# Mixed values turned by VectorE's 32x32 block transposes and by 128-byte stores, instead of on TensorE

## Chip, cores and metric

The kernel runs on one core of a Trainium2 chip. The metric is the device time of one execution in microseconds; a version is told by the median of its runs. All data are f32 (products are made of a high and a low part in a reduced f32 format, three matrix products each).

## What is computed

One layer of a hybrid encoder on 1024 tokens of width 1024. Eight heads of width 128 produce the 1024 mixed values of a token: four heads of gated linear attention (GLA) and four of differential attention. Each head's output is normalised over its 128 values and gated. Then the output projection reads all of them, with the features as the contracted dimension:

```python
o_gla = head_rmsnorm(o_gla, gla_norm_w[l]) * silu(ggate)            # (B, S, 4, 128)
o_diff = head_rmsnorm(o_diff, diff_norm_w[l]) * (1.0 - lam_init) * silu(dgate)
mixed = concatenate([o_gla.reshape(B, S, 512), o_diff.reshape(B, S, 512)], axis=-1)
x = x + mixed @ w_out[l]
hc = rmsnorm(x, norm_cross_w[l])
x = x + cross_attention(hc, rmsnorm(mem, norm_mem_w[l]), w_cq[l], w_ckv[l], w_co[l])
return rmsnorm(x, final_norm_w)
```

## The kernel before

Everything is ordered by one hand-written list, PLAN: `stages()` builds it and `with_weights()` puts the loads of weight tiles between. Each engine walks the whole list and issues its part of every stage, so the order on an engine, and on its DMA queue, is the order of the list. Semaphores tie the engines together.

The tokens are tiled by 128 (TT = 8 tiles). After the gate preparation come GLA_STEPS = 16 steps (two head pairs, eight tiles each), then DIFF_STEPS = 32 steps (four heads, eight tiles each), then the cross-attention keys K and values V of the memory, then the output projection X in seven products of half-size blocks, then the cross attention (Q, SC, PT, O), its output projection Y and the final norm. TensorE projects the next steps' inputs (proj, proja, projb) between the small products of a step, as its filler.

How a mixed value travels. In a GLA step s TensorE leaves the output of a head pair in PSUM (stage o), VectorE sums it into o_f, ScalarE squares it (osq), VectorE and GpSimd make the inverse norm (ovar; POOL's line L997), and VectorE multiplies norm and gate in (stage ofin, L1598) and writes 128 tokens x 256 features to a half of mix_out. SP stores it to the HBM scratch `mixed`, laid out token by feature, in rows of 1 KB (L961). mix_out has two halves, so ofin(s) waits for the store of step s-2. A differential step i does the same with 128 x 128 values (PV, pvvar, pvfin at L1696, L967, rows of 512 bytes) and four quarters of mix_out.

The output projection wants features on the partitions. So from the last quarter of the differential steps on, ScalarE's queue loads `mixed` back, a tile of 128 tokens x 512 features at a time (stage loadm, L1362, into one of two halves of tile_a, rows of 2 KB), TensorE transposes it in four 128x128 pieces into a PSUM bank (stage MT, by `turn`, L1932), and ScalarE copies the bank to mixT, scaled by the head norm's weight (L1111). There are 16 such tiles: MT(t, 0) of the GLA features and MT(t, 1) of the differential ones. The tile MT(t, 0) stands between proja and proj of a differential step from i = 22 on, seven of them; the nine others stand between the K and V stages. loadm of tile n + 2 stands directly behind MT of tile n. xa stages then split mixT into high and low parts, and asum stages add blocks of it, on VectorE and by GpSimd's accumulating DMAs.

Other users of the queues: SP's queue also loads every weight tile (w, L921, 256 KB, a ring of four raw tiles and 13 split ones) and the residual tiles (loadx); GpSimd's queue adds up blocks of the output weights in HBM during the GLA steps (out_sums, one 1 MB transfer per step for 11 steps, issued behind the inverse norm) and of the cross output weights during the differential steps (late_sums, every second step).

On VectorE a GLA step is, in order: sc_lo (stage sc), the state and its low part (kv), var_o (ovar), q_lo and k_lo (qk), ke_lo (kdT), ofin of the step before, v and gate of the next projection (proj, gmul), w_lo of a weight tile, the masked scores (scp), o_f (o). A differential step is: row maximum of the next scores (max), var_o, the low parts of the transposed map (T) and of the next queries and keys (TQK), pvfin of the step before, w_lo, the map (comb), v, gate and rope of a later projection (proj), pv_f (PV).

Transposes go to PSUM banks in turn, kept in order by `rings`: TR numbers the stages T, MT, HT and PT, TURN_ACT all of them but MT, whose copy is counted by ring_raw. `turned_out` makes TensorE wait until VectorE has read the earlier ones.

Of the kernel before, what the change touches and what calls it, by code (L numbers as in the profile page):

```python
# [32 lines left out]
P = 128  # L33
# [13 lines left out]
NEG = -1e30  # L47

# [79 lines left out]
def stages():  # L128
# [41 lines left out]
    plan.append(("ofin", GLA_STEPS - 1))  # L170
# [12 lines left out]
    for i in range(last):  # L183
# [12 lines left out]
        if i + 3 < DIFF_STEPS:  # L196
# [14 lines left out]
    plan.extend([*turned_maps(last), ("pvvar", last - 1), ("K", 2), ("pvfin", last - 1), ("Ke", 2)])  # L211
    plan.extend(turned_tile(n_turned))
    n_turned += 1
    plan.extend([("K", 3), ("Ke", 3), *turned_tile(n_turned), ("PV", last), ("pvvar", last), ("pvfin", last)])
# [217 lines left out]
TR = rings({"T", "MT", "HT", "PT"})  # L432


TURN_ACT = rings({"T", "HT", "PT"})
# [7 lines left out]
def ring_bank(stage):  # L443

    if stage[0] == "T":
        return 6 + stage[2]
    return 7 if stage[0] == "MT" and not stage[2] else 6 + TR[stage] % 2

# [70 lines left out]
def build(nc, a, out):  # L519

    with ExitStack() as ctx:
# [67 lines left out]
        mix_out = sb("mix_out", [P, 512], F32, part1)  # L589
# [81 lines left out]
        mixed = nc.dram_tensor("mixed", (S, D), F32, kind="Internal").ap()  # L671
# [11 lines left out]
        d_mixg = [sem(f"gla_mix_stored{j}") for j in range(2)]  # L683
        d_mixd = [sem(f"diff_mix_stored{j}") for j in range(4)]
# [45 lines left out]
        ring_raw = sem("mixed_tiles_kept")  # L730
        sum_dve = sem("weight_sums")
# [115 lines left out]

        def ring_job(stage):
# [10 lines left out]
            c = cols(t if kind == "MT" else t % 4)  # L859
# [45 lines left out]
        def _(sp):  # L905
# [39 lines left out]
            for stage in PLAN:  # L945
# [11 lines left out]
                elif kind == "ofin":  # L957
                    s = w[0]
                    p, t = divmod(s, TT)
                    sp.wait_ge(of_dve, at("ofin", s))  # L960
                    sp.dma_start(mixed[cols(t), 256 * p:256 * p + 256],  # L961
                                 mix_out[:, 256 * (s % 2):256 * (s % 2) + 256]).then_inc(d_mixg[s % 2], 16)
                elif kind == "pvfin":
                    i = w[0]
                    h, t = divmod(i, TT)
                    sp.wait_ge(pf_dve, at("pvfin", i))
                    sp.dma_start(mixed[cols(t), GH * GDV + P * h:GH * GDV + P * h + P],  # L967
                                 mix_out[:, P * (i % 4):P * (i % 4) + P]).then_inc(d_mixd[i % 4], 16)
# [1296 lines left out]
```

## Time and profile before

| | us |
|---|---|
| median of 3 runs (824.53 to 827.13) | 825.1 |
| the profiled execution | 825.03 |
| its span | 823.3 |

| engine | busy us | share of the span |
|---|---|---|
| PE (TensorE matmul) | 809.1 | 98% |
| DVE (VectorE) | 574.7 | 70% |
| ACT (ScalarE) | 430.6 | 52% |
| POOL (GpSimd) | 85.7 | 10% |
| DMA queue of SP (q1) | | 24.5% of 16 engines |
| DMA queue of POOL (q0) | | 19.6% of 16 engines |

All times in the profile count from the span's start. A row of a timeline is one instruction or a merged run of equal ones, with its start and duration, and in brackets how long the engine had idled before and who released it. The chain that ended last is followed back from the last instruction, at each step to what released it; an engine that fills the chain is the bound there. The granted clock of TensorE is at its full level over nearly the whole span. The GLA steps run from about 83 to 205 us, the differential ones to 485, K and V to 518, X to about 612.

### The profile page before, as it was taken

The numbers are of one execution on the slowest core, as the hardware profiler recorded it, in microseconds if no ns is written. First come the engines' busy times: TensorE is split into PE (matmuls) and PEld (weight loads), VectorE is DVE, ScalarE is ACT, GpSimd is POOL, SyncE is SP. The second block draws the span as 40 slices with busy tenths as digits, with TensorE's granted clock in tenths as the row PEclk, the third lists the DMA queues.
The fourth block names the chain that finished last, engine by engine and source line by source line (L and its number), as shares of the span: only waits on it lengthen the run. The fifth ranks groups of instructions, "written<-read, shape, count | busy, mean of one in ns | idle before, by whom it ended". The sixth has DMA issues, their size and how long they took to land.

```text
span 823.3 us, 12950 instructions
## 1 busy us (share of the span) xinstructions
PE 809.1 (98%) x4472; PEld 678.9 (82%) x4472; DVE 574.7 (70%) x1330; ACT 430.6 (52%) x1041; POOL 85.7 (10%) x122
## 2 busy tenths in 40 slices
PE   8999999999999999999999999999999999999996
PEld 7878888887788888888888898888888888888885
DVE  6688566665678668767757877599836454367997
ACT  6775445443455445445546576644645454366443
POOL 3100122211010111111000001010110000001201
PEclk9999999999999999999999999999999999999999
DMA  8321369952223255545512178954422111206945
GB/s 292 115 83 39 91 192 205 193 121 65 87 88 109 84 99 109 114 84 122 108 63 74 58 227 248 295 124 124 150 81 77 39 64 52 78 13 143 216 91 204
DMA packets 70408, 99.19 MB, mean 120 GB/s; under 512 B 6596, under 2 KB 38472, under 8 KB 70344
## 3 DMA queue, kind: packets, MB, share of 16 engines
q1 hardware_dynamic: 52360, 64.29, 24.5%
q0 software_dynamic: 15392, 29.36, 19.6%
q10 hardware_dynamic: 2592, 4.72, 1.7%
q8 instruction: 36, 0.59, 0.3%
q14 instruction: 28, 0.23, 0.1%
HBM read 83.68 MB, written 31.46 MB: 140 GB/s over the span
## 4 chain that ended last, share of the span: by engine, by line
PE 90%; DVE 7%; ACT 2%; issue 1%; DMA 0%; POOL 0%; ACTq 0%; DVEq 0%
PE bank L1860 14%; PE bank L1862 14%; PE bank L1861 14%; PE banks2to L1860 10%; PE banks2to L1862 10%; PE banks2to L1861 10%; PE banks6to L1932 4%; PE banks2to L2126 3%; PE bank L2149 2%; DVE neg_max L1659 2%; DVE w_lo L1395 1%; PE banks2to L2066 1%; PE bank L2151 1%; DVE prT_lo L1394 1%; DVE actT_lo L1394 1%
## 5 line engine op out<-in xcount | busy, mean ns | idle before, releaser
L1862 PE MATMUL bank<-w_hi,actT_lo 128*128 128x512 f32 x412 | 161.4, 392 | 0.0
L1860 PE MATMUL bank<-w_hi,actT_hi 128*128 128x512 f32 x384 | 154.9, 403 | 0.7 <-DVE gate L1549 0.4
L1861 PE MATMUL bank<-w_lo,actT_hi 128*128 128x512 f32 x384 | 149.6, 390 | 0.0
L1395 DVE SCALAR_TENSOR_TENSOR w_lo<-w_raw,vecs,w_hi 128x512 fp32r<-128x512 f32 x120 | 86.8, 749 | 27.2 <-ACT w_hi L1111 27.2
L1862 PEld LDWEIGHTS bank<-w_hi,actT_lo 128*128 128x128 f32 x412 | 77.3, 188 | 17.1
L1111 ACT ACTIVATE w_hi<-w_raw,vecs 128x512 fp32r<-128x512 f32 x120 | 82.5, 720 | 7.1 <-DMA w_raw<-in_w_ckv 3.8
L1860 PEld LDWEIGHTS bank<-w_hi,actT_hi 128*128 128x128 f32 x384 | 72.1, 188 | 16.2 <-DVE w_lo L1395 1.5
L1861 PEld LDWEIGHTS bank<-w_lo,actT_hi 128*128 128x128 f32 x384 | 72.3, 188 | 12.9
L997 POOL TENSOR_TENSOR rs_o<-var_o,neg_half 128x1 f32<-128x1 f32 (+1 forms) x48 | 31.1, 647 | 369.1 <-DVE var_o L1686 256.8
L1862 PE MATMUL banks2to<-w_hi,actT_lo 128*128 128x512 f32 x164 | 64.0, 390 | 0.0
L1278 ACT ACTIVATE prob<-banks2to,neg_maxs 128x128 f32<-128x128 f32 (+7 forms) x64 | 46.9, 740 | 15.1 <-DVE neg_maxs L1660 15.0
L1111 ACT ACTIVATE w_hi<-w_raw 128x512 fp32r<-128x512 f32 x56 | 33.8, 627 | 36.5 <-DMA w_raw<-out_sums 13.3
L1659 DVE TENSOR_REDUCE neg_max<-banks2to 128x2 f32<-128x256 f32 (+8 forms) x33 | 43.4, 1316 | 4.4 <-PE banks2to L2131 4.0
L1860 PE MATMUL banks2to<-w_hi,actT_hi 128*128 128x512 f32 x112 | 44.7, 399 | 0.0
L1861 PE MATMUL banks2to<-w_lo,actT_hi 128*128 128x512 f32 x112 | 43.7, 390 | 0.0
L1394 DVE TENSOR_TENSOR w_lo<-w_raw,w_hi 128x512 fp32r<-128x512 f32 x56 | 37.2, 685 | 9.0 <-ACT w_hi L1111 9.0
L1860 PE MATMUL banks2to<-actT_hi,w_hi 128*128 128x512 f32 (+1 forms) x100 | 39.6, 396 | 1.6 <-DVE w_lo L1395 1.6
L1111 ACT ACTIVATE qk_tok<-bank 128x192 f32<-128x192 f32 x27 | 8.9, 331 | 56.9 <-PE bank L1862 56.9
L1812 DVE TENSOR_REDUCE x_negmax<-banks2to 128x4 f32<-128x1024 f32 x8 | 9.8, 1223 | 41.1 <-PE banks2to L1862 41.1
L1862 PE MATMUL banks2to<-actT_hi,w_lo 128*128 128x512 f32 (+1 forms) x100 | 38.3, 383 | 0.0
L1861 PE MATMUL banks2to<-actT_lo,w_hi 128*128 128x512 f32 (+1 forms) x100 | 38.2, 382 | 0.0
L2149 PE MATMUL bank<-dv,prT_hi 128*128 128x256 f32 x144 | 35.3, 325 | 1.4 <-DVE qkT_lo L1394 0.7
(373 smaller groups left out, 2009.7 us busy)
## 6 DMA issues: line engine op xcount, KB each, us to landing
w_raw<-in_w_in SPq DMA_DIRECT2D x56, 256.0 KB, 3.8
out_sums<-in_w_out POOLq DMA_DIRECT2D x11, 1024.0 KB, 10.0
late_sums<-in_w_co POOLq DMA_DIRECT2D x11, 1024.0 KB, 9.0
w_raw<-in_w_ckv SPq DMA_DIRECT2D x32, 256.0 KB, 3.4
w_raw<-in_w_cq SPq DMA_DIRECT2D x32, 256.0 KB, 2.7
stage_in<-in_x SPq DMA_DIRECT2D x8, 512.0 KB, 4.6
tile_a<-mixed ACTq DMA_DIRECT2D x16, 256.0 KB, 3.4
x_res<-in_x SPq DMA_DIRECT2D x8, 512.0 KB, 6.8
```

Of the source, the lines that this page charges most:

```text
L997: pool.tensor_tensor(dst, src, neg_half[:, 0:n], ALU.pow).then_inc(sem_out, 1)
L1111: return act.activation(dst, src, ACT.Copy, scale=scale)
L1278: last = act.activation(prob[:, m, 0:n], wide[:, 2 * m:2 * m + 2, :].rearrange("p j c -> p (j c)")[:, 0:n], ACT.Exp, scale=DQK ** -0.5, bi ...
L1394: return dve.tensor_tensor(dst, src, hi.bitcast(F32), ALU.subtract)
L1395: return dve.scalar_tensor_tensor(dst, src, scale, hi.bitcast(F32), ALU.mult, ALU.subtract)
L1659: then_wait(dve.tensor_reduce(neg_max[:, i % 2, m], both[:, m, :], AX.X, ALU.max, negate=True))
L1860: pe.matmul(dst, l_hi, r_hi, start=start, stop=False)
L1861: pe.matmul(dst, l_hi, r_lo, start=False, stop=False)
L1862: return pe.matmul(dst, l_lo, r_hi, start=False, stop=stop)
L1932: last = pe.transpose(ps[:, cols(j)], src, ident[:, :])
L2126: last = pe.matmul(wide[:, 2 * half + g // 512, 0:keys.stop - g], l[rows, 0, cols(t)], r[rows, 1, keys], start=m == 0, stop=m == 2 and key ...
L2149: pe.matmul(bank1[:, 0:256], prT_hi[:, b, :], dv2[:, v, :, :].rearrange("p a c -> p (a c)"), start=b == 0, stop=False)
```

## The change

The scratch `mixed` is laid out feature by token. Behind each ofin and pvfin there is a new stage, oturn or pvturn: VectorE turns the product within 32x32 blocks into the new tile mix_t, and SP stores it in four transfers, one for each band of 32 partitions (32 tokens). In a transfer, row r of block b goes to feature 32 b + r, and its 32 tokens are a run of 128 bytes in HBM. A GLA step stores 1024 such runs, a differential step 512, where 128 rows were stored before. mix_out and mix_t have 256 columns each, where mix_out had 512. For GLA both are one buffer: ofin(s) waits for oturn(s-1), and oturn(s) for the landed store of step s-1. For the differential steps both have two.

oturn(s-2) stands behind sc(s), pvturn(i-1) ahead of PV(i). At the end of the GLA steps the order is oturn(14), ofin(15), oturn(15). The tile MT is loaded as 512 rows of 512 bytes, already turned, and ScalarE copies it from tile_a to mixT; TensorE has no part in MT any more, and the rings number T, HT and PT alone.

```diff
+BLK = 32
+STORED = 16 * P // BLK
...
         plan.append(("sc", s))
+        plan.extend([("oturn", s - 2)] if s > 1 else [])
...
-    plan.append(("ofin", GLA_STEPS - 1))
+    plan.extend([("oturn", GLA_STEPS - 2), ("ofin", GLA_STEPS - 1), ("oturn", GLA_STEPS - 1)])
...
+        plan.extend([("pvturn", i - 1)] if i else [])
         if i == last - 2:
...
-TR = rings({"T", "MT", "HT", "PT"})
-TURN_ACT = rings({"T", "HT", "PT"})
+TR = rings({"T", "HT", "PT"})
...
-        mix_out = sb("mix_out", [P, 512], F32, part1)
+        mix_out = sb("mix_out", [P, 256], F32, part1)
+        mix_t = sb("mix_t", [P, 256], F32, part1)
...
-        mixed = nc.dram_tensor("mixed", (S, D), F32, kind="Internal").ap()
+        mixed = nc.dram_tensor("mixed", (D, S), F32, kind="Internal").ap()
...
+        def turned_rows(first, n, t, band):
+            tokens = slice(P * t + BLK * band, P * t + BLK * band + BLK)
+            return mixed[first:first + n, tokens].rearrange("(b r) c -> r b c", r=BLK)
+        def turned_blocks(first, n, band):
+            return mix_t[BLK * band:BLK * band + BLK, first:first + n].rearrange("r (b c) -> r b c", c=BLK)
...
 SP:
-                elif kind == "ofin":
+                elif kind == "oturn":
                     s = w[0]
                     p, t = divmod(s, TT)
-                    sp.wait_ge(of_dve, at("ofin", s))
-                    sp.dma_start(mixed[cols(t), 256 * p:256 * p + 256],
-                                 mix_out[:, 256 * (s % 2):256 * (s % 2) + 256]).then_inc(d_mixg[s % 2], 16)
+                    sp.wait_ge(mg_dve, s + 1)
+                    for a4 in range(P // BLK):
+                        sp.dma_start(turned_rows(256 * p, 256, t, a4),
+                                     turned_blocks(0, 256, a4)).then_inc(d_mixg, 16)
 (pvfin becomes pvturn in the same way, with d_mixd[i % 2])
...
                 elif kind == "loadx":
                     if w[0] == 4:
-                        sp.wait_ge(pf_dve, DIFF_STEPS)
+                        sp.wait_ge(md_dve, DIFF_STEPS)
...
 ScalarE, MT:
-                    act.wait_ge(ring_pe, TR[stage] + 1)
+                    act.wait_ge(d_tile[n % 2], 16 * (n // 2 + 1))
...
+                    loaded = tile_a[:, 512 * (n % 2):512 * (n % 2) + 512].rearrange("p (j c) -> p j c", j=4)
+                    copy(mixT[:, 4 * kk:4 * kk + 4, cols(t)], loaded,
...
 ScalarE, loadm:
-                        act.wait_ge(ring_pe, TR[RELOADS[n - 2]] + 1)
+                        act.wait_ge(ring_raw, n - 1)
...
+                    rows = mixed[512 * kk:512 * kk + 512, cols(t)].rearrange("(j p) c -> p j c", p=P)
...
 VectorE:
                 elif kind == "ofin":
-                    if s >= 2:
-                        dve.wait_ge(d_mixg[j], 16 * (s // 2))
+                    wait(dve, mg_dve, s)
...
+                elif kind == "oturn":
+                    s = w[0]
+                    dve.wait_ge(of_dve, s + 1)
+                    wait(dve, d_mixg, STORED * s)
+                    dve.transpose(mix_t[:, :], mix_out[:, :]).then_inc(mg_dve, 1)
+                elif kind == "pvturn":
+                    i = w[0]
+                    dve.wait_ge(pf_dve, i + 1)
+                    if i < 2:
+                        dve.wait_ge(d_mixg, STORED * GLA_STEPS)
+                    else:
+                        dve.wait_ge(d_mixd[i % 2], STORED * (i // 2))
+                    dve.transpose(mix_t[:, cols(i % 2)], mix_out[:, cols(i % 2)]).then_inc(md_dve, 1)
...
 TensorE:
-                elif kind == "MT":
-                    n = RELOAD[stage]
-                    pe.wait_ge(d_tile[n % 2], 16 * (n // 2 + 1))
-                    turn(stage, [tile_a[:, cols(4 * (n % 2) + j)] for j in range(4)])
```

## Rows read from the trace of the kernel before

**Rows 1.** The page: busy time of TensorE, and the chain's shares by engine.

```profile
PE 809.1 (98%) x4472; PEld 678.9 (82%) x4472; DVE 574.7 (70%) x1330; ACT 430.6 (52%) x1041; POOL 85.7 (10%) x122
...
PE 90%; DVE 7%; ACT 2%; issue 1%; DMA 0%; POOL 0%; ACTq 0%; DVEq 0%
```

**Rows 2.** Busy time by stretch: GLA steps, 130 to 170 us, differential steps, keys and values.

```profile
core 0: us, PE busy (x) PEld busy (x) DVE busy (x) ACT busy (x) POOL busy (x), PEclk, DMA share, GB/s
90.00:210.00 120.00, 118.97 (x668) 98.25 (x668) 76.21 (x237) 53.92 (x189) 23.61 (x27) 1.00 0.67 150
130.00:170.00 40.00, 39.38 (x229) 32.65 (x228) 25.94 (x81) 18.14 (x62) 9.90 (x11) 1.00 1.01 195
210.00:485.00 275.00, 272.73 (x1698) 229.08 (x1697) 200.04 (x586) 141.92 (x411) 27.10 (x43) 1.00 0.41 98
485.00:515.00 30.00, 30.00 (x176) 26.02 (x175) 23.89 (x35) 20.09 (x36) 2.65 (x2) 1.00 0.81 250
```

**Rows 3.** DMA queues (packets, MB, share): 130 to 170 us, then 180 to 220.

```profile
q0 software_dynamic: 2741, 5.42, 80.2%
q1 hardware_dynamic: 4018, 2.35, 20.5%
...
q1 hardware_dynamic: 3755, 2.10, 19.2%
```

**Rows 4.** The chain in order of time: start us, us charged, what (a stage MT).

```profile
442.74 0.44 PE banks6to L1932 x4
```

**Rows 5.** VectorE's timeline in a differential step.

```profile
448.25 1.76 DVE L1659 TENSOR_REDUCE neg_max<-banks2to 128x2 f32<-128x1536 f32 x1 [0.17 <-PE banks2to L2131]
```

**Rows 6.** ScalarE's copies of MT, and the landing of their loads.

```profile
L1111 ACT ACTIVATE mixT<-banks6to,scale_neg x8: 670/682/704, 401.0 to 515.1; 128x512 f32<-128x512 f32 x8
...
DMA to landing us min/median/max: 2.5/3.4/6.8
```

**Rows 7.** VectorE's timeline in a GLA step.

```profile
124.38 0.42 DVE L1394 TENSOR_TENSOR v<-bank,v 128x256 fp32r<-128x256 f32 x1 [1.36 <-ACT tanh_g L1186]
...
128.57 0.28 DVE L1394 TENSOR_TENSOR q_lo<-q_dec,q_hi 128x128 fp32r<-128x128 f32 x1
...
129.67 0.61 DVE L1598 SCALAR_TENSOR_TENSOR mix_out<-o_f,rs_o,gate 128x128 f32<-128x128 f32 x2 [0.61 <-POOL rs_o L997]
131.52 0.42 DVE L1394 TENSOR_TENSOR v<-bank,v 128x256 fp32r<-128x256 f32 x1 [1.24 <-ACT tanh_g L1186]
```

**Rows 8.** The chain in order of time, two long differential steps.

```profile
385.45 0.34 DVE pv_f L1680
...
457.72 2.04 DVE neg_max L1659
```

**Rows 9.** Landing of stores into mixed: 90-165, 165-210, 210-490 us; those of 101.1, 145.0.

```profile
DMA to landing us min/median/max: 2.4/5.9/11.3
...
DMA to landing us min/median/max: 1.8/1.8/5.1
...
DMA to landing us min/median/max: 1.6/1.6/9.5
...
DMA to landing us min/median/max: 6.3/6.3/6.3
...
DMA to landing us min/median/max: 6.5/6.5/6.5
```

**Rows 10.** SP's issue of a transfer in pieces of 64 bytes (duration in ns).

```profile
L938 SPq DMA_DIRECT2D ga_raw<-in_w_in x1: 447/447/447, 5.8 to 5.8; - x1
```

**Rows 11.** VectorE's and TensorE's timelines at the end of the GLA steps.

```profile
205.04 0.61 DVE L1598 SCALAR_TENSOR_TENSOR mix_out<-o_f,rs_o,gate 128x128 f32<-128x128 f32 x2
205.57 0.41 DVE L1659 TENSOR_REDUCE neg_max<-banks2to 128x2 f32<-128x256 f32 x1
...
209.13 0.42 DVE L1394 TENSOR_TENSOR qkT_lo<-banks6to,qkT_hi 128x256 fp32r<-128x256 f32 x1
...
209.71 0.39 PE L2126 MATMUL banks2to<-qkT_hi 64*128 64x256 f32 x2
```

More of the change, by code:

```diff
@@ L210, in stages @@
             plan.append(("PV", i))
-    plan.extend([*turned_maps(last), ("pvvar", last - 1), ("K", 2), ("pvfin", last - 1), ("Ke", 2)])
+    plan.extend([*turned_maps(last), ("pvvar", last - 1), ("K", 2), ("pvfin", last - 1), ("Ke", 2), ("pvturn", last - 1)])
     plan.extend(turned_tile(n_turned))
     n_turned += 1
-    plan.extend([("K", 3), ("Ke", 3), *turned_tile(n_turned), ("PV", last), ("pvvar", last), ("pvfin", last)])
+    plan.extend([("K", 3), ("Ke", 3), *turned_tile(n_turned), ("PV", last), ("pvvar", last), ("pvfin", last), ("pvturn", last)])
     n_turned += 1
@@ L446, in ring_bank @@
         return 6 + stage[2]
-    return 7 if stage[0] == "MT" and not stage[2] else 6 + TR[stage] % 2
+    return 6 + TR[stage] % 2
 RELOADS = [stage for stage in PLAN if stage[0] == "MT"]
@@ L682, in build @@
         d_raw = [sem(f"weight_loaded{j}") for j in range(NRAW)]
-        d_mixg = [sem(f"gla_mix_stored{j}") for j in range(2)]
-        d_mixd = [sem(f"diff_mix_stored{j}") for j in range(4)]
+        d_mixg = sem("gla_mix_stored")
+        d_mixd = [sem(f"diff_mix_stored{j}") for j in range(2)]
         d_tile = [sem(f"mixed_tile_loaded{j}") for j in range(2)]
@@ L1690, in _ @@
                     dve.wait_ge(pv_pool, i + 1)
[L1691 to L1692 removed]
+                    if i < 2:
+                        dve.wait_ge(mg_dve, GLA_STEPS)
                     else:
[L1694 removed]
+                        dve.wait_ge(md_dve, i - 1)
                     c = slice(P * (i % 4), P * (i % 4) + P)
[L1696 removed]
+                    dve.scalar_tensor_tensor(mix_out[:, cols(i % 2)], pv_f[:, i % 2, :], rs_o[:, i % 2, 0:1], gate[:, c],
                                              ALU.mult, ALU.mult).then_inc(pf_dve, 1)
@@ L1908, in late_bank @@
                 return banks[LATE_BANK[stage]]
-            kept = [0]
             def turned_out(n):
-                mixed_tiles = sum(stage[0] == "MT" for stage in list(TR)[:n])
-                wait(pe, ring_dve, n - mixed_tiles)
-                if mixed_tiles > kept[0]:
-                    kept[0] = mixed_tiles
-                    pe.wait_ge(ring_raw, mixed_tiles)
+                wait(pe, ring_dve, n)
             def turn(stage, parts):
@@ L2196, in _ @@
                     open_already = kind == "Q" and ("Qa", *w) in NTH
-                    pe.wait_ge(ring_dve, TURN_ACT[("HT", 4 * half + 3, 0 if kind == "Qa" and h + d == 0 else 1)] + 1)
+                    pe.wait_ge(ring_dve, TR[("HT", 4 * half + 3, 0 if kind == "Qa" and h + d == 0 else 1)] + 1)
                     ps = banks[LATE_BANK[job]] if open_already else late_bank(job)
```

39 lines of the change are left out of this document (16 added, 23 removed).

## The prediction

> **What bounds the kernel now.** I read the page from the top. TensorE is busy 98% of the span, and the chain that ended last is TensorE for 90% and VectorE for 7% [rows 1]. The table by stage shows how little it idles: 118.97 of 120 us busy in the GLA steps, 272.73 of 275 in the differential ones, 30.00 of 30 while the memory keys and values are projected [rows 2]. So TensorE work that goes away is time saved, as long as nothing else becomes late by as much, and VectorE is the only engine that already is late here and there. The DMA engines matter for what follows: 0.67 of them are busy over the GLA steps and 1.01 from 130 to 170 us, where GpSimd's queue alone holds 80.2% and SP's 20.5% [rows 2, 3].
>
> The sum is made against the profiled execution: 825.03 us, span 823.3 and 1.7 around it. The median of the runs is 825.1, so the two are the same for this purpose.
>
> **Removed: the transposes on TensorE.** Sixteen MT stages of four 128x128 transposes go. Transposes overlap their neighbours, so I don't take their durations but what the chain of work charges TensorE for one stage of four, 0.44 us [rows 4]. 16 x 0.44 = 7.0 us. Nine of them lie behind 475 us, where TensorE is busy all the time; seven lie from 400 to 452 us, and in the last three of these steps VectorE has only 0.17 us idle ahead of a row maximum [rows 5]. There I count nothing for three, so 13 x 0.44 = **-5.7 us** (-3.5 to -7.0).
>
> **MT on ScalarE.** The copy reads SBUF instead of PSUM (0.68 us before [rows 6], SBUF hardly slower) and waits for the load itself; the next load waits for that copy. This puts some 0.4 us of idle into ScalarE per tile, 14 times. ScalarE is busy 20 of 30 us there [rows 2], so I cost it at nothing. If that cover were gone it would be up to 14 x 0.4 = 5.6 us. The reload keeps its bytes with 512 pieces of 512 bytes in place of 128 of 2 KB; it landed in 2.5 to 6.8 us [rows 6], with two stages of the fill between issue and use. Nothing, with up to 1 us as the other end.
>
> **Added on VectorE, differential steps.** A pvturn per step, one 128x128 instruction. The trace has no block transpose; the nearest rows are subtractions, 0.28 us for 128x128 and 0.42 for 128x256 [rows 7]. I take 0.3 (0.15 to 1.2: half of it, and four passes). In most steps it falls into idle time before the row maximum. Where the step is long it doesn't: the chain of 384 to 391 us runs through VectorE's rope sum, the reduction pv_f, ScalarE's square of it, w_hi, w_lo and the maximum without a gap [rows 8], and pvturn stands exactly ahead of pv_f. The same chain comes at this step of the two heads before, near 250 and 318 us, and the maximum at 457.72 starts one that holds to 470, with two pvturns on it. 5 x 0.3 = **+1.5 us** (+0.5 to +6). Stores here have two buffers, so a store has two steps to land in; the slowest took 9.5 us [rows 9], and 32 steps in 275 us are 8.6 each. No wait.
>
> **Added at the end of the GLA steps.** ofin(15) needs mix_out free, so oturn(14) stands directly ahead of it, and oturn(15) directly behind must wait until the store of step 14 has landed in HBM, since mix_t has one buffer. SP issues four transfers for it: 0.45 us each (the nearest issue of short pieces took 0.447), and a store landed 1.8 us after issue at this quiet place [rows 9, 10]. From 205.04 us, where ofin stood, that is 0.42 for oturn(14), 3 x 0.45 + 1.8 = 3.15 until the last transfer has landed, and 0.42 for oturn(15): VectorE comes to max(0) at 209.0 instead of 205.57, 3.5 us late. Queued behind it are max(0), E(0) on ScalarE, comb(0) and the lo part of the next keys at 209.13. TensorE starts S(1) at 209.71, 0.16 us after that lo part ends, with its filler used up [rows 11]. So nearly all of it shows: **+3.5 us** (+1.5 to +7).
>
> **Added in each GLA step.** This is the term in doubt. Before, mix_out had two halves and a store two steps. Now oturn(s) waits until the store of step s-1 has landed, one step earlier. A step is 7.1 us (the values of two projections start at 124.38 and 131.52). Behind oturn VectorE still does the state, the lo parts and ofin until 130.3, then idles 1.24 us until the values of the next projection [rows 7]. Less 0.42 for the transpose, 0.8 us of delay is free; beyond that v, gate and with them TensorE's next products slip. So a store may take 7.1 + 0.8 from one oturn to the next. It takes 0.42 + 3 x 0.45 + its landing, so a landing above 6.2 us is paid for. Before, ten stores from 90 to 165 us landed in 2.4 to 11.3 us, median 5.9, the other six mostly in 1.8 [rows 9]. Issued one by one, three took 6.2 to 6.3, one, the longest, 11.3 and the next 6.5 [rows 9]; with nothing added these are 0.1 + 0.1 + 5.1 + 0.3 = 5.6 us over the limit. Then there are 64 pieces per DMA engine and step instead of 8. SP's pieces took 19.2% of 16 x 40 us / 3755 = 33 ns at a mean of 560 bytes from 180 to 220 us [rows 3]; in proportion to bytes that is 8 ns for one of 128, at most the same 33: 0.5 to 2.1 us, less 0.3 for the eight that go. With 0.7 each, the five are 9 us over it. Against that, a step that slips lets GpSimd's stream drain. I take **+6 us**, near the lower of the two (0 if the new place of the stores, 3 us earlier in the step, misses the stream; up to 20 below).
>
> The Trainium skill, in "DMA: Bandwidth & Descriptors" under Specifications, puts a line at 512 bytes for full rate, below which a DMA engine reads, modifies and writes. That speaks against this change: its pieces are 128 bytes in place of 512 and 1024. No row here shows a store below 512 bytes. The slow-store rival below is what it would do.
>
> **SP's queue.** A step's store is four issues, 4 x 0.45 = 1.8 us in place of one, and stands behind sc (GLA) or proj (differential), ahead of the weight loads that follow in the plan; the wait for VectorE that SP does there delays them too. In a GLA step one weight tile is loaded, and the ring is filled tiles ahead, so I cost it at nothing; up to 1.4 us per group change, seven of them, if a load is what VectorE's w_lo waits for.
>
> **Sum.** 825.0 - 5.7 + 1.5 + 3.5 + 6 = **830.3 us**, its own range 826 to 837.
>
> **The rivals.**
> 1. *The stores hide.* oturn never waits in a GLA step; only the end of these steps and the transposes are paid. 825.0 - 5.7 + 1.5 + 3.5 = 824.3 us (822.6 to 827). For it: landings of 2.4 to 4.3 in four of ten stores. Against: the DMA engines are full from 130 to 170 us.
> 2. *Faster: TensorE's share comes back whole.* Also the wait behind oturn(14) is short or covered and transposes cost 0.2: 825.0 - 7.0 + 1.0 + 1.0 = 820.0 us. It decides if S(1) has slack or SP issues the four in a fraction of 0.45. Against: TensorE starts S(1) within 0.2 us of its operand [rows 11].
> 3. *Short pieces are slow.* From 130 to 170 us a piece of GpSimd's stream took 80.2% of 16 x 40 / 2741 = 187 ns [rows 3]. If each short piece has to let one of these pass, 64 x 0.19 = 12 us per step in place of 7.1 + 0.8, so about 4 us over six steps, 24, and the early steps some more in part; the same follows if a piece of 128 bytes costs several times its share. 824.3 + 24 = 848 us.
> 4. *It does not do what it says*: the TensorE rows with tile_a stay in number before 515 us. The edits delete them, so no chance is kept for it.
>
> **How the numbers follow.** The forecast 0.43, rival 1 0.28, rival 2 0.12, rival 3 0.17. A change below 0.3% (2.5 us: 822.6 to 827.6) can't be told from none. Faster: rival 2 whole and 0.06 of rival 1, 0.18. Same: 0.21 of rival 1 and 0.04 of the forecast, 0.25. Slower: 0.57. The range 821 to 846 leaves out half of each outer rival.
>
> **What would show it.** The four transposes per MT gone and TensorE busy about 7 us less. VectorE idle ahead of its transposes, released by the DMA into mixed: about 3 us once near 205 us, and some of 1 to 5 us from 100 to 180 us; without these, rival 1. The stretch from the first GLA step to 210 us longer by 4 to 10 us, the stretch from 475 to 520 shorter by some 4. The transpose at 0.3 and 0.42 us. Landing of the new stores: below 6 us everywhere speaks for rival 1, above 10 in most steps for rival 3. The forecast is wrong if TensorE's idle time in the GLA steps grows by less than 3 us or more than 15.

## The result, and the profile after

The changed kernel takes 837.8 us (median; 835.2 to 838.5), the kernel before 824.9 in the same rounds: ratio 1.0147, 95% interval 1.0135 to 1.0159. The forecast was 830.3, range 821 to 846. The sign was right, the size was not: 12.1 us (1.0147 x 824.9 - 824.9) where 5.3 were forecast. TensorE has 64 instructions fewer [rows 1] and the span is still 12.8 us longer. From the page of the changed kernel, the busy times and the chain:

```profile
PE 807.5 (97%) x4408; PEld 675.7 (81%) x4408; DVE 585.2 (70%) x1378; ACT 431.0 (52%) x1041; POOL 85.8 (10%) x122
...
PE 82%; DVE 8%; DMA 4%; ACT 3%; issue 2%; SPq 1%; ACTq 0%; DVEq 0%
```

TensorE's busy time fell by 1.6 us, not by 7, and the chain of waits now has 4% of DMA in it. The table by stretch (columns as in [rows 2]; the last stretch is 5 us longer):

```profile
90.00:210.00 120.00, 112.79 (x622) 93.46 (x621) 76.81 (x235) 52.44 (x179) 23.64 (x27) 0.97 0.71 148
130.00:170.00 40.00, 34.16 (x184) 28.03 (x182) 22.54 (x69) 14.93 (x50) 9.40 (x10) 0.91 0.96 177
210.00:485.00 275.00, 269.17 (x1621) 223.66 (x1621) 202.15 (x619) 135.09 (x403) 26.04 (x41) 0.99 0.41 90
485.00:520.00 35.00, 32.85 (x212) 28.84 (x210) 26.27 (x45) 25.45 (x46) 2.45 (x3) 1.00 0.72 209
```

TensorE idles 5.8 of 40 us where it idled 0.6, the granted clock is 0.91 there instead of 1.00, and it now idles 2.15 us while the memory keys and values are projected.

**Where the time goes, by marks.** The order of the work is the same in both kernels, so the same instruction can be looked up in both, and the difference of its starts says how late the changed kernel is at that point. VectorE's timeline (start us, duration, ...): in the kernel before, the values of the last GLA projection, the third row maximum, the 24th, the last, and the first variance behind the output projection:

```profile
190.01 0.42 DVE L1394 TENSOR_TENSOR v<-bank,v 128x256 fp32r<-128x256 f32 x1 [1.27 <-ACT tanh_g L1186]
218.45 0.95 DVE L1659 TENSOR_REDUCE neg_max<-banks2to 128x2 f32<-128x768 f32 x1
396.25 2.29 DVE L1659 TENSOR_REDUCE neg_max<-banks2to 128x2 f32<-128x2048 f32 x1 [0.68 <-PE banks2to L2131]
467.17 1.21 DVE L1659 TENSOR_REDUCE neg_max<-banks2to 128x1 f32<-128x1024 f32 x1
591.04 0.14 DVE L1807 TENSOR_SCALAR var_x<-sq_x 128x1 f32<-128x1 f32 x1
```

and the same five in the changed kernel:

```profile
198.76 0.42 DVE L1409 TENSOR_TENSOR v<-bank,v 128x256 fp32r<-128x256 f32 x1 [0.45 <-ACT tanh_g L1200]
232.27 0.95 DVE L1686 TENSOR_REDUCE neg_max<-banks2to 128x2 f32<-128x768 f32 x1
410.57 2.29 DVE L1686 TENSOR_REDUCE neg_max<-banks2to 128x2 f32<-128x2048 f32 x1 [0.49 <-PE banks2to L2148]
478.13 1.22 DVE L1686 TENSOR_REDUCE neg_max<-banks2to 128x1 f32<-128x1024 f32 x1
603.88 0.14 DVE L1834 TENSOR_SCALAR var_x<-sq_x 128x1 f32<-128x1 f32 x1
```

The differences are 8.75, 13.82, 14.32, 10.96 and 12.84 us, so the five stretches cost +8.75, +5.07, +0.50, -3.36 and +1.88. From there to the last instruction nothing changes in any run; in e1 and e12 below the span ends 0.9 us later behind that instruction than in the others, which no mark shows.

| stretch | forecast | measured |
|---|---|---|
| GLA steps (to 190 us) | +6 | +8.75 |
| end of GLA, first maxima (to 218) | +3.5 | +5.07 |
| 22 differential steps (to 396) | +1.5 with the next | +0.50 |
| steps with seven reloads (to 467) | 4 x -0.44 = -1.76 | -3.36 |
| keys, values, output projection (to 591) | 9 x -0.44 = -3.96 | +1.88 |

(The forecast's four and nine are stages at 0.44 us; behind 475 us it counted only them.) The largest miss is the last row, 5.8 us; the first two together miss 4.3.

**The waits.** VectorE's waits of the changed kernel (us in total, times, the longest):

```profile
DVE mix_t L1619 <- DMA mixed<-mix_t: 13.9, 4, 7.3
```

Its 16 GLA transposes by their line (duration in ns, min, median, max):

```profile
L1619 DVE STREAM_TRANSPOSE mix_t<-mix_out x16: 435/438/446, 97.8 to 217.6; 128x256 f32<-128x256 f32 x16
```

Two of the four that waited for a store, from the timeline:

```profile
149.51 0.45 DVE L1619 STREAM_TRANSPOSE mix_t<-mix_out 128x256 f32<-128x256 f32 x1 [7.31 <-DMA mixed<-mix_t]
217.57 0.45 DVE L1619 STREAM_TRANSPOSE mix_t<-mix_out 128x256 f32<-128x256 f32 x1 [2.27 <-DMA mixed<-mix_t]
```

The other two waits were 1.98 us at 121.81 and 2.30 at 188.65. Over the first of these the values stay within 0.91 us of the kernel before, over the one of 7.31 they go from 0.36 to 6.34 us late, over the last from 8.05 to 9.25 and back to 8.75. The store that the transpose at 149.51 waits for lies in the stretch from 130 to 150 us. The DMA queues there (packets, MB, share), then the landing of SP's stores:

```profile
q0 software_dynamic: 1317, 2.60, 72.5%
q1 hardware_dynamic: 4288, 1.31, 30.3%
```

```profile
DMA to landing us min/median/max: 1.5/9.4/11.1
```

GpSimd's queue holds 72.5% of the 16 engines, and SP's pieces fill the rest.

**The clock.** What I had not counted is that TensorE is slow behind these stalls. Its timeline at the second row maximum, then the table by stretch around both stalls:

```profile
218.12 0.39 PE L1889 MATMUL bank<-w_hi,actT_lo 128*128 128x512 f32 x1
221.94 0.39 PE L2143 MATMUL banks2to<-qkT_hi 64*128 64x256 f32 x2 [3.43 <-DVE qkT_lo L1409]
...
223.16 0.63 PE L1888 MATMUL banks2to<-w_lo,actT_hi 128*128 128x512 f32 x1
```

```profile
152.00:157.00 5.00, 4.45 (x17) 3.63 (x17) 4.02 (x12) 2.31 (x8) 1.39 (x2) 0.50 0.64 92
...
218.00:222.00 4.00, 0.57 (x5) 0.15 (x3) 2.41 (x11) 2.25 (x9) 0.00 (x0) 1.00 0.22 35
222.00:226.00 4.00, 4.00 (x17) 3.20 (x18) 2.42 (x10) 1.91 (x6) 0.00 (x0) 0.58 0.24 63
226.00:230.00 4.00, 4.00 (x19) 3.23 (x19) 1.39 (x6) 0.39 (x1) 0.00 (x0) 0.99 0.26 66
```

After 3.43 us of idle the granted clock is 0.5 of full speed (1.2 instead of 2.4 GHz) for some 4 us, and a matmul that took 0.39 us takes 0.63. The second row maximum is 11.27 us late (222.78 against 211.51), the third 13.82. The same follows the stall near 150 us: the values at 146.60 before are 6.34 late, those at 153.65 then 8.04. Here no run holds the clock up, so how much of the 1.7 us is the clock isn't shown. In e8, whose only change lies 60 us later, the same two are 6.97 and 8.12 late.

**Behind 485 us.** The chain of waits from 483 to 530 us in the changed kernel (start, us charged, what; a part of it):

```profile
487.88 4.16 DMA w_raw<-in_w_ckv
492.07 0.74 ACT w_hi L1125
492.83 1.43 DVE w_lo L1410 x2
494.27 6.21 DMA w_raw<-in_w_ckv
...
501.13 0.72 ACT mixT L1125
...
506.13 1.22 DVE mixT L1666
...
509.03 3.71 DMA w_raw<-in_w_ckv
...
517.30 5.35 DMA w_raw<-in_w_ckv
522.67 0.73 ACT w_hi L1125
523.43 0.76 DVE w_lo L1410
524.23 0.50 PE banks2to L1887
```

This is a ring: SP may load a raw weight tile when VectorE has made the lo part of the tile four before, the load takes 3.7 to 6.2 us, ScalarE and VectorE split it, and that frees the next. Between two loads the chain also runs through what stands ahead of the split on these engines: ScalarE's copy of a reloaded tile (mixT, L1125) and VectorE's sum of two blocks (L1666). In the kernel before the chain of this stretch is TensorE from end to end.

### The profile page after: what moved, and what is told of

Same layout as the page of the kernel before. It is cut to its first block, busy times and chain, and to the rows that moved or that the text cites. A ratio compares the mean times of both kernels' runs of the same rounds, so it can differ in the third digit from the quotient of the medians.

```text
span 836.1 us, 13037 instructions
## 1 busy us (share of the span) xinstructions
PE 807.5 (97%) x4408; PEld 675.7 (81%) x4408; DVE 585.2 (70%) x1378; ACT 431.0 (52%) x1041; POOL 85.8 (10%) x122
## 4 chain that ended last, share of the span: by engine, by line
PE 82%; DVE 8%; DMA 4%; ACT 3%; issue 2%; SPq 1%; ACTq 0%; DVEq 0%
PE bank L1887 13%; PE bank L1889 13%; PE bank L1888 13%; PE banks2to L1887 9%; PE banks2to L1889 9%; PE banks2to L1888 9%; PE banks6to L1949 3%; PE banks2to L2143 3%; DMA w_raw<-in_w_ckv 2%; DVE w_lo L1410 2%; PE bank L2166 2%; DMA mixed<-mix_t 1%; DVE neg_max L1686 1%; PE banks2to L2083 1%; PE bank L2168 1%
## 5 line engine op out<-in xcount | busy, mean ns | idle before, releaser
L1125 ACT ACTIVATE w_hi<-w_raw,vecs 128x512 fp32r<-128x512 f32 x120 | 82.8, 720 | 13.0 <-DMA w_raw<-in_w_ckv 9.0
L1125 ACT ACTIVATE w_hi<-w_raw 128x512 fp32r<-128x512 f32 x56 | 33.7, 627 | 37.8 <-DMA w_raw<-out_sums 13.5
L1121 ACT ACTIVATE junk<-pv_f 128x128 bf16<-128x128 f32 x32 | 9.9, 310 | 54.4 <-DVE pv_f L1707 54.4
L1889 PEld LDWEIGHTS banks2to<-w_hi,actT_lo 128*128 128x128 f32 x164 | 31.2, 190 | 6.7
```

Source lines behind the costliest of these rows:

```text
L1125: return act.activation(dst, src, ACT.Copy, scale=scale)
L1889: return pe.matmul(dst, l_lo, r_hi, start=False, stop=stop)
```

## The experiments

The runs of one batch share the runs of the kernel before (825.2, 824.9 and 825.0 us). "Late at the marks" is the difference over the five stretches, as above, in the profiled execution.

| run | median us | ratio, interval | GLA | to 218 | to 396 | to 467 | to 591 |
|---|---|---|---|---|---|---|---|
| changed kernel | 837.8 | 1.0147, 1.0135-1.0159 | +8.75 | +5.07 | +0.50 | -3.36 | +1.88 |
| e1 four buffers | 825.9 | 1.0006, 0.9997-1.0015 | -0.04 | +0.94 | +0.57 | -3.36 | +2.54 |
| e2 long stores | 830.7 | 1.0068, 1.0054-1.0081 | +0.97 | +5.98 | +0.54 | -3.37 | +0.88 |
| e3 long reloads | 836.3 | 1.0126, 1.0111-1.0142 | +8.50 | +5.07 | +0.55 | -3.35 | +1.46 |
| e4 TensorE only | 821.9 | 0.9954, 0.9941-0.9966 | -0.03 | +0.03 | +0.04 | -3.55 | +0.42 |
| e5 GLA values only | 821.8 | 0.9965, 0.9953-0.9978 | 0.00 | 0.00 | +0.01 | -3.54 | -0.25 |
| e6 e4, later rows | 820.2 | 0.9947, 0.9935-0.9959 | +0.02 | -0.01 | +0.04 | -3.54 | -0.92 |
| e7 e4, no reloads | 819.4 | 0.9932, 0.9920-0.9943 | 0.00 | 0.00 | -0.03 | -3.54 | +0.11 |
| e8 busy TensorE | 834.8 | 1.0127, 1.0109-1.0146 | +8.63 | +3.30 | +0.58 | -3.36 | +3.46 |
| e9 no sums | 828.8 | 1.0044, 1.0032-1.0055 | -0.01 | +6.15 | +0.51 | -3.33 | +2.41 |
| e10 whole, mended | 823.0 | 0.9974, 0.9964-0.9984 | 0.00 | 0.00 | +0.58 | -3.35 | +1.66 |
| e11 e5, later rows | 820.7 | 0.9951, 0.9938-0.9963 | 0.00 | 0.00 | +0.01 | -3.55 | -0.31 |
| e12 e1, long late pieces | 824.9 | 1.0001, 0.9992-1.0010 | -0.04 | +0.92 | +0.52 | -3.36 | +0.76 |

The GLA mark is taken from the first GLA step (81.37 us before); up to there a run starts up to 0.6 us earlier or later. Stretches in which two runs do the same agree within 0.1 us, with waits of microseconds in them within 0.3. The last stretch is the exception: runs alike in all that touches it (the changed kernel, e1, e8, e9) give 1.9 to 3.5. So the profiles say nothing there below about 1.5 us, and small differences are read from the medians. The marks are those of one execution, which need not be near the median: that of e8 took 837.1 us, and those of e7, e9 and e10 were the slowest of their runs (821.2, 830.4 and 824.1). In e2, e3, e4, e6, e7, e9 and e12 something is left out or lands elsewhere, so they don't compute the layer; the others do.

### Is it the single buffer, the piece size, or GpSimd's stream?

**e1.** Four buffers for the transposed GLA values:

```
-                    wait(dve, d_mixg, STORED * s)
-                    dve.transpose(mix_t[:, :], mix_out[:, :]).then_inc(mg_dve, 1)
+                    if s >= 4:
+                        dve.wait_ge(d_mixg[s % 4], STORED * (s // 4))
+                    dve.transpose(tile_a[:, 256 * (s % 4):256 * (s % 4) + 256], mix_out[:, :]).then_inc(mg_dve, 1)
```

> The changed kernel with four buffers for the transposed GLA values in place of one (they lie in the SBUF of tile_a, which is unused until the reloads), so that a transpose waits for the store of four steps before; everything else, the 128-byte pieces too, stays. Theory A (the single buffer): the lines of the two traces drift apart by 8.75 us over the GLA steps and by 5.1 us more over the first two row maxima, all of it at transposes that waited for a store and at TensorE's slow stretch right behind them. It goes: 837.8 - 13.8 = 824 us, VectorE has no wait for DMA ahead of a GLA transpose. Rival B (the short pieces load the DMA engines, whatever waits for them): the weights and GpSimd's stream are late too, the GLA steps stay 3 us or more longer than before, 828 to 834 us.

825.9 us: theory A, 12 us back (1.9 us short of the 824 expected; in its profiled execution 0.94 of that lies at the first maxima and 0.9 at the end of the span). The stores from 130 to 150 us land as late as before:

```profile
DMA to landing us min/median/max: 7.8/8.9/10.7
```

Nobody waits for them any longer: VectorE's list of waits from 84 to 225 us has no DMA. SP's issues of these transfers got long too, 0.46 to 5.05 us with a median of 1.74 (0.30 to 2.03 with a median of 0.78 in the changed kernel, both from 130 to 150 us), where the forecast had 0.45 each. The 0.94 us left at the first maxima are about the two transposes ahead of max(0), 2 x 0.44; in e10, which moves them, nothing is left.

**e2.** The same four transfers of a store in long rows:

```
-                        sp.dma_start(turned_rows(256 * p, 256, t, a4),
-                                     turned_blocks(0, 256, a4)).then_inc(d_mixg, 16)
+                        sp.dma_start(mixed[P * t + BLK * a4:P * t + BLK * a4 + BLK, 256 * p:256 * p + 256],
+                                     mix_t[BLK * a4:BLK * a4 + BLK, 0:256]).then_inc(d_mixg, 16)
```

> The changed kernel, but the four transfers of a store write 32 rows of 1 KB (GLA) or 512 bytes (differential) in place of 128-byte pieces: same bytes, same four issues, same single buffer and waits; the values land in another place, so what is computed from them is not the reference's, and the reloads read other rows in pieces of 512 bytes as before. Theory A (a store is late because it is issued behind GpSimd's stream and waited for one step later; the size of its pieces hardly matters): the long wait near 150 us and the one behind oturn(14) stay, 834 to 839 us. Rival B (the small pieces are what takes long): the waits in the GLA steps fall below 1 us in all, 824 to 829 us.

830.7 us, between the two expectations: both are half wrong. VectorE's waits for stores, all of the run:

```profile
DVE mix_t L1619 <- DMA mixed<-mix_t: 7.7, 5, 2.6
```

and the landing of the stores from 130 to 150 us:

```profile
DMA to landing us min/median/max: 2.0/3.5/5.8
```

Five waits and none above 2.6 us where one of 7.3 stood, a median landing of 3.5 us instead of 9.4, and the GLA steps are 0.97 us late, not 8.75: the size of the pieces is most of that term. The end of the GLA steps is no better than with short pieces (+5.98 against +5.07): there the wait is four issues and one landing. VectorE's wait is even a little shorter, 1.89 us against 2.27, but the granted clock stays at 0.50 to 0.71 from 212 to 220 us, where the changed kernel has its low stretch for some 4 us; e9 has the same (+6.15, a wait of 2.03 us, 0.50 to 0.76 from 212 to 220).

**e9.** GpSimd's accumulating transfers left out (and SP's waits for the sums that they would have made), the single buffer and the short pieces kept:

```
-                    if w[0] < len(OUT_ADDENDS):
+                    if w[0] < 4:
```

> The changed kernel without GpSimd's seven accumulating transfers of 1 MB in the GLA steps (the four that start the sums stay; the sums of the output weights are incomplete, so the result is not the reference's). Single buffer, short pieces and waits stay. Theory A2 (a store of 128-byte pieces is only late when it stands in the same DMA engines as GpSimd's stream): nearly all of the 8.75 us of the GLA steps goes, waits of VectorE for a store there below 1 us in all, the 5.1 us at the first two row maxima stay: 837.8 - 8 = 829.5 us, 828.5 to 831. Rival (they are slow by themselves): 834 us or more.

828.8 us, as theory A2 has it. All waits for stores in the run:

```profile
DVE mix_t L1619 <- DMA mixed<-mix_t: 2.0, 1, 2.0
```

The one left is that of oturn(15), and the short pieces land quickly once the stream is gone (130 to 190 us):

```profile
DMA to landing us min/median/max: 1.5/1.7/3.0
```

So the 8.75 us need three things at once: one buffer, pieces of 128 bytes and the stream. Without any one of them they shrink to 1 us or nothing (e1, e2, e9). Two or three buffers were not tried.

### The clock at the end of the GLA steps

**e8.** TensorE kept busy in its idle time:

```
+                    for _ in range(28 * (i == 1)):
+                        pe.transpose(banks[6][:, 0:P], ident[:, :], ident[:, :])
                     pe.wait_ge(tq_dve, i + 1)
```

> The changed kernel with 28 transposes of the identity on TensorE (0.11 us each, 3.1 in all) ahead of the first wait of S(1), in the 3.43 us that TensorE idles near 220 us; nothing reads them. There the granted clock fell to 0.50 for some 4 us after the idle stretch and a matmul of 128x512 took 0.63 instead of 0.39 us. Theory H (the second row maximum is late by 2.55 us more because of this clock): the clock stays at 1.00 and about 2.5 us come back, 835.3 us. Rival: it is late because of what VectorE or ScalarE do, and the time stays at 837.8, or is longer if the transposes end behind the operand.

834.8 us, ratio 1.0127 against 1.0147: 1.6 us back, not 2.5, and the two intervals overlap; the marks decide. The transposes fill the gap, the matmuls behind it keep 0.39 us and the clock stays at 1.00. TensorE's timeline of this run, then its table by stretch:

```profile
217.65 3.22 PE L2133 MATMUL banks6to<-ident 128*128 128x128 f32 x28
221.07 0.39 PE L2145 MATMUL banks2to<-qkT_hi 64*128 64x256 f32 x2 [0.20 <-DVE qkT_lo L1409]
...
222.07 0.39 PE L1888 MATMUL banks2to<-w_lo,actT_hi 128*128 128x512 f32 x1
```

```profile
222.00:226.00 4.00, 4.00 (x21) 3.23 (x20) 2.39 (x8) 2.29 (x7) 0.00 (x0) 1.00 0.09 25
```

The stretch to 218 us falls from 5.07 to 3.30: 1.8 us of it were the clock. The other 3.3 are the wait itself, close to the 3.5 of the forecast. Of the 2.55 us between the second and the third maximum 0.97 stay at full clock (10.40 to 11.37 us late in e8); that part theory H had wrong. The late stretch of this run is the worst of all (+3.46), with the clock at 0.83 from 520 to 530 us; that is why its marks add up to only 0.8 us less than the changed kernel's (12.05 against 12.84).

### Why nine of the sixteen stages gave nothing

**e4.** The kernel before with TensorE's part alone:

```
-                elif kind == "MT":
-                    n = RELOAD[stage]
-                    pe.wait_ge(d_tile[n % 2], 16 * (n // 2 + 1))
-                    turn(stage, [tile_a[:, cols(4 * (n % 2) + j)] for j in range(4)])
```

> The kernel before, with only TensorE's part of the change: the transposes MT are left out and ScalarE copies the reloaded tile as it is (untransposed, so what is computed from it is not the reference's); stores, reloads and VectorE as before. The forecast's term: 13 of 16 stages at 0.44 us, 825 - 5.7 = 819.3 us. Theory D (TensorE runs into the pace of the weights behind 485 us, and only the seven stages before give time): the lines gain 3.3 us by 460 us and nothing or a loss after it, 821 to 822.5 us. Rival E (the loss behind 485 us is made by the stores and their place in SP's queue): the whole share, 818 to 819.5 us.

821.9 us, theory D. Seven stages give 3.55 us, 0.51 each, also the three that the forecast left out because VectorE had 0.17 us of slack [rows 5]; the nine behind give nothing (+0.42). From 500 to 510 us, first the kernel before, then e4, by the table of stretches:

```profile
500.00:510.00 10.00, 10.00 (x48) 8.15 (x47) 8.45 (x13) 6.17 (x12) 1.35 (x1) 1.00 0.86 256
```

```profile
500.00:510.00 10.00, 7.90 (x34) 5.72 (x33) 8.28 (x12) 5.91 (x10) 1.35 (x1) 1.00 1.03 285
```

What ScalarE waits for from 470 to 530 us, first the kernel before, then e4:

```profile
ACT w_hi L1111 <- DMA w_raw<-in_w_ckv: 3.8, 5, 1.4
```

```profile
ACT w_hi L1108 <- DMA w_raw<-in_w_ckv: 8.4, 7, 2.8
```

TensorE and the ring of weights were about level before. Shorten TensorE, and it waits for the ring. e5, below, says the same from the other side: it keeps eight of the nine late stages on TensorE, is busy 10.00 of 10 us there, and ends the stretch no later than e4 without them (-0.25 against +0.42).

**e6 and e7** ask what holds the ring: the shared DMA engines or its four tiles. e6 loads two residual rows later, e7 leaves the last seven reloads out:

```
-        if n in (3, 4):
-            plan.append(("loadx", n + 1))
...
-    plan.extend([("loadx", 6), ("loadx", 7)])
+    plan.extend([("loadx", 4), ("loadx", 5), ("loadx", 6), ("loadx", 7)])
```

```
-                    act.dma_start(tile_a[:, 512 * (n % 2):512 * (n % 2) + 512],
+                    if n < TT + 1:
+                      act.dma_start(tile_a[:, 512 * (n % 2):512 * (n % 2) + 512],
```

> The TensorE-only kernel (MT's transposes left out, so what is computed is not the reference's), and the residual rows 4 and 5, 512 KB each, are loaded after the memory values instead of among their weights. In that kernel TensorE idles 2.1 us between 500 and 510 us for w_lo, where the DMA engines are busy all the time. Theory F (the weights of the memory values share full DMA engines): 1 to 2 us come back, 820 to 821 us. Rival G (the ring of four raw tiles sets the pace: a load is only issued when VectorE has made the lo part of four tiles before): as without it, 821.5 to 822.3 us.

> The TensorE-only kernel, and the last seven reloads are left out too (ScalarE copies what is in tile_a; what is computed is not the reference's): 1.8 MB less on the DMA engines between 475 and 520 us. Theory F (the weights of the memory keys and values share full DMA engines with the reloads): they arrive earlier and up to all of the 4 us that TensorE lost behind 475 us come back, 818.5 to 820.5 us. Rival G (the ring of four): 821.5 to 822.3 us.

820.2 and 819.4 us against 821.9. The intervals of e6 and e4 overlap, so e6 alone doesn't carry it; those of e7 and e4 touch only at the edge. Between e4 and e7 lie 2.5 us by the medians and 1.8 by the ratios, of the 4 looked for: the direction of theory F. But e7 also takes the copies' waits for their loads and seven issues of 0.33 us from ScalarE, and one such copy and its issue stand in the chain of e4 near 488 us, so that the shared DMA engines alone are not shown to be the cause. The rest stays open between the ring's own round trip, which no run changed (a fifth tile, or the copies and sums in another place), and the clock. The profile of e7 shows the clock: TensorE waits once for w_lo there, and 0.83 is granted from 500 to 510 us. The profiled execution of e7 took 821.2 us, the slowest of its six, which is why its last stretch in the table (+0.11) is worse than its median. TensorE's wait from 465 to 530 us, then the stretch:

```profile
PE banks2to L1860 <- DVE w_lo L1395: 1.8, 1, 1.8
```

```profile
500.00:510.00 10.00, 8.17 (x29) 6.18 (x28) 8.97 (x13) 5.34 (x10) 2.65 (x2) 0.83 1.01 277
```

**e3 and e12** ask what the short pieces add there. In e3 the reloads read rows of 2 KB; in e12, which is e1 with more, the differential stores are in rows of 512 bytes too:

```
-                    rows = mixed[512 * kk:512 * kk + 512, cols(t)].rearrange("(j p) c -> p j c", p=P)
+                    rows = mixed[cols(t % 4), 512 * kk:512 * kk + 512]
```

```
-                        sp.dma_start(turned_rows(GH * GDV + P * h, P, t, a4),
-                                     turned_blocks(P * (i % 2), P, a4, mix_t)).then_inc(d_mixd[i % 2], 16)
+                        sp.dma_start(mixed[GH * GDV + P * h + BLK * a4:GH * GDV + P * h + BLK * a4 + BLK, cols(t)],
+                                     mix_t[BLK * a4:BLK * a4 + BLK, cols(i % 2)]).then_inc(d_mixd[i % 2], 16)
```

> The changed kernel, but each reload reads 128 rows of 2 KB in place of 512 pieces of 512 bytes (other values, so what is computed from them is not the reference's); stores, waits and order stay. Behind the last attention step the changed kernel loses 1.8 us against the kernel before where 4.0 were forecast to be gained. Theory C (the reload's short pieces delay the weights of the memory keys and values): up to 3 us come back, 834 to 836 us, and TensorE waits less for w_lo between 486 and 526 us. Rival D (the weights are late because SP issues the stores' four transfers ahead of them, or TensorE only runs into the pace of its weights): the same as the changed kernel, 837 to 839 us.

> The four-buffer kernel of the first experiment (825.9 us), but the differential values are stored in rows of 512 bytes and the reloads read rows of 2 KB (other places and values, so the result is not the reference's); four issues per store, waits and order stay. Theory F (short pieces take DMA time that the late weights need): of the 2.35 us that this kernel loses behind 467 us up to 2 come back, as in the TensorE-only kernel, which loses 0.4: 824 to 824.6 us. Rival (the loss is VectorE's transposes and SP's four issues): 825.4 to 826.3 us.

e3: 836.3 us. By the marks the last stretch is 0.4 us shorter, which is within what alike runs differ by, and its interval overlaps that of the changed kernel; no verdict. e12: 824.9 us against e1's 825.9, the intervals overlap, and 0.76 instead of 2.54 us at the marks. This leans to theory F with about 1 us in place of 2 and doesn't settle it.

### A version that beats both

**e5.** Only the GLA values are transposed by VectorE, out of two halves of mix_out into four buffers; the last two transposes stand in the pause between the first maximum and its sums; the differential values stay as they were, since their eight reloads all lie behind 467 us:

```
-    plan.extend([("S", 0), ("max", 0), ("E", 0), ("comb", 0)])
+    plan.extend([("S", 0), ("max", 0), ("oturn", GLA_STEPS - 2), ("oturn", GLA_STEPS - 1), ("E", 0), ("comb", 0)])
...
+                    if kk:
                         _, _, ps = ring_job(stage)
                         act.wait_ge(ring_pe, TR[stage] + 1)
+                    else:
+                        n = RELOAD[stage]
+                        act.wait_ge(d_tile[n % 2], 16 * (n // 2 + 1))
```

> The kernel before with the change made for the GLA values alone: VectorE transposes them out of two halves of mix_out into four buffers (in the SBUF of tile_a), they are stored by feature in 128-byte pieces, and the eight reloads of them go to ScalarE without TensorE; the differential values keep their stores by token and their transposes on TensorE. The last two transposes stand between the first row maximum and its exponential's sums, where VectorE waits for ScalarE. By what the four-buffer run and the TensorE-only run showed: 0 in the GLA steps, 0 to 1 at the first two maxima, 3.5 us gained from the seven reloads before 460 us, nothing lost behind 485 us: 825.2 - 3.5 = 821.7 us, up to 822.7. Rival: the 128-byte stores of the GLA values slow the weights all the same, 824 us or more.

821.8 us, 0.35% under the kernel before, with no loss at any mark. Both transposes of the end are free where they stand; VectorE's timeline:

```profile
205.58 0.91 DVE L1630 STREAM_TRANSPOSE tile_a<-mix_out 128x256 f32<-128x256 f32 x2
207.16 0.75 DVE L1420 SCALAR_TENSOR_TENSOR w_lo<-w_raw,vecs,w_hi 128x512 fp32r<-128x512 f32 x1 [0.67 <-ACT w_hi L1127]
```

**e10** is the whole change with these cures and e6's later rows; **e11** is e5 with e6's later rows.

> The whole change with what the runs so far point to: four buffers for the transposed GLA values, the last two GLA transposes between the first row maximum and its sums, and the residual rows 4 and 5 loaded after the memory values; the differential values transposed by VectorE too. From the lines of the earlier runs: 0 in the GLA steps and at the first maxima, 0.5 us for 32 transposes, 3.5 gained by 460 us, behind 485 us between 0 and 1.5 lost (TensorE's share is eaten by the wait for weights, 0.9 gained with the later rows, 1 to 1.5 lost to the short pieces): 822.2 us, 821 to 824. Rival: without the 8.75 us of waits the short pieces no longer matter anywhere and TensorE's nine late stages pay too, 818 to 820 us.

> The kernel with GLA values alone by VectorE (821.75 us) with the residual rows 4 and 5 loaded after the memory values. There TensorE is busy 10.00 of 10 us from 480 to 530 us, so weights that come earlier have nothing to give: 821.2 to 822.2 us. Rival: what is left of its waits for w_lo goes as well, 820.5 to 821 us.

e10: 823.0 us, within its expectation: the whole change can be made 0.26% faster than the kernel before, but its second half costs more (0.58 of VectorE's transposes, and the late stretch, +1.66 against -0.31 in e11) than it gives; its interval doesn't meet that of e11. e11: 820.7 us, in the range of its rival, the fastest kernel here that does the whole computation, 0.49% under the kernel before; its interval reaches into that of e5, and the marks show no difference (-0.31 against -0.25), so the extra 1 us is not shown.

## Why the prediction was wrong in size

**TensorE's share, -5.7: the step that failed.** "Nine of them lie behind 475 us, where TensorE is busy all the time" was right as a reading and wrong as a conclusion. Those nine gave nothing (e4: +0.42 instead of -3.96), because the weights are level with TensorE there. The profile before had a sign of it, unread: ScalarE waits 3.8 us in five times for the weights of that stretch. The seven stages before gave 0.48 to 0.51 us each instead of the four counted: for those three I let VectorE's 0.17 us of slack bound the gain. Net by e4: forecast -5.7, got -3.55 + 0.42 = -3.1. Against the forecast the nine stages are 4.4 us off and the seven 1.8 us the other way; with the terms below (+1.5, +2.75, +1.6, -0.8) that is the 7.5 us by which the marks (12.84) pass the forecast 5.3.

**The late stretch, an effect not in the sum.** Beyond the missing gain the changed kernel loses there: 1.88 us against e4's 0.42. That difference alone is no more than alike runs differ by, but all four alike runs lie above e4 (1.88 to 3.46), and so does e10 (1.66) above e6 (-0.92), which loads the rows at the same place. SP's queue was costed at nothing and the reload's pieces at 0 to 1 us. Short pieces beside the weights are the likely cause (e12, e3 lean to it), VectorE's transposes and SP's four issues are not excluded. The cause stays open.

**The GLA steps, +6: measured 8.75.** The mechanism was right, and its three conditions are shown (e1, e2, e9). It came mostly as one wait of 7.3 us; the rows had one landing of 11.3 us too, 5.1 of the 5.6 us that the forecast found over its limit. Another 1.7 us come right behind it, where the clock is at 0.50 (6.34 to 8.04 us late); the forecast had no term for that, and no run separates it. The +6 was a choice between 0 and 20, so that it came this near is in part luck. I had noted that a slipping step lets the stream drain; it did: from 150 to 152 us the engines' share is 0.28.

**The end of the GLA steps, +3.5: measured 5.07.** The wait was read right (3.3 us with the clock held up, e8); 1.8 us are the clock.

**VectorE's transposes, +1.5: measured 0.7**, 0.50 over 22 steps and 0.19 in the next ten (-3.36 against e4's -3.55). The duration was as taken (min, median, max in ns):

```profile
L1627 DVE STREAM_TRANSPOSE mix_t<-mix_out x32: 301/304/313, 239.0 to 496.3; 128x128 f32<-128x128 f32 x32
```

About half as many steps as I had named let it through.

**ScalarE, 0: confirmed before 467 us**, where e4 loses nothing. The copy takes 0.71 to 0.72 us from SBUF instead of 0.68 [rows 6]. Behind 485 us a copy stands in the chain (501.13 above), so there the term is not shown to be nothing.

**The rivals.** Rival 1 (the stores hide) and rival 2 (TensorE's share comes back whole) are excluded by the 7.3 us wait and by e4. Rival 3, priced at 24 us more, had the right ingredient: without short pieces the GLA steps lose 0.97 us (e2). It wrongly charged each step; three of the sixteen transposes waited in those steps. The forecast cited for it the Trainium skill, "DMA: Bandwidth & Descriptors", Specifications: below 512 bytes an engine reads, modifies and writes. e2 against the changed kernel agrees with that in direction (landing 3.5 instead of 9.4 us); no run here shows what an engine does with such a piece. Where the engines are free no effect is seen: the stores from 200 to 225 us land in a median of 1.7 us, those of before in 1.8 [rows 9].

**What was to show it.** TensorE's busy time fell by 1.6 us and not by 7, because a matmul at 1.2 GHz counts 0.63 instead of 0.39 us (in e1, without the two stalls, it fell by 6.2, to 802.9); the VectorE wait at the end was 2.3 us and not 3; 485 to 520 us got longer, not shorter by 4. TensorE's idle time in the table from 90 to 210 us grew by 6.2 us (118.97 to 112.79), inside the bounds of 3 and 15.

## What to carry to other kernels

A stretch in which TensorE is busy all the time is not proof that its work is worth time: look at what the other engines wait for in it, and if a ring of loads is level with TensorE, work taken from TensorE turns into a wait for the ring. Before a store must land within one step, compare the worst landing with the step (here 11 us against 7), above all with small pieces beside a stream; four buffers, in SBUF that was unused at that time, gave 12 us here. A slow stretch can follow a TensorE stall of some microseconds: here one of 3.43 us cost 1.8 us more.

## What the runs showed that I had not expected

- The granted clock fell to 0.50 after TensorE idled 3.43 us near 220 us, for some 4 us, and after the stall near 150 us for about 6. The first cost 1.8 us (e8); behind the second 1.7 us more were lost, not shown to be all the clock. The length of one wait doesn't decide it: in e7 one of 1.83 us was followed by 0.50 from 506 to 508 us (0.83 over 10 us), while in e1 one of 2.34 us, up to 495.82, left the clock at 1.00, and so did the changed kernel's idle time of 2.57 of 10 us from 520 to 530 us, in several pieces.
- Transfers of 32 KB in 128-byte pieces landed in a median of 9.4 us beside GpSimd's stream, in 1.7 us with the stream left out, and in 3.5 us beside it in rows of 1 KB.
- VectorE's block transpose of 128x256 takes 0.44 us, of 128x128 0.30, about as a subtraction of that shape [rows 7].
